# Group norm and key norm of an RWKV-7 layer on one core: head sums as one product with a pair matrix, roots as logarithm and exponential on ScalarE

## The reference

```python
kk = split_heads((k * k_k).astype(f32), N_MAIN_HEADS)
kk = kk * lax.rsqrt(jnp.maximum(jnp.sum(kk * kk, -1, keepdims=True), 1e-24))
...
mean = jnp.mean(y, -1, keepdims=True)
var = jnp.mean(jnp.square(y - mean), -1, keepdims=True)
yn = ((y - mean) * lax.rsqrt(var + GN_EPS)).reshape(bsz, t, D_MAIN)
```

## Time and profile before

| | us |
|---|---|
| median of 3 runs | 3013.67 (3013.06 to 3025.93) |
| the profiled execution | 3011.51 |
| its span in the trace | 3009.5 |
| of this, PE busy | 2826.8 (94%) |
| ACT busy | 1065.8 (35%) |
| DVE busy | 1565.1 (52%) |
| POOL busy | 1209.2 (40%) |

### The profile page before, as it was taken

One profiled execution on the slowest core, in us unless ns is written; L12 is line 12 of the kernel. 1 busy time (PEld: TensorE's weight loads), 2 busy tenths in 40 slices (PEclk: granted clock), 3 DMA queues, 4 the chain that ended last, 5 costly groups with the idle time before them and its releaser, 6 DMA issues. The chain is left out here.

```text
span 3009.5 us, 55580 instructions
## 1 busy us (share of the span) xinstructions
PE 2826.8 (94%) x23253; PEld 2278.6 (76%) x23253; DVE 1565.1 (52%) x2118; ACT 1065.8 (35%) x1870; POOL 1209.2 (40%) x1140
## 2 busy tenths in 40 slices
PE   7999789989879999999999999988889999999998
PEld 6888567777757788888887777756667788888887
DVE  6233456656452754445225778867653745445222
ACT  3111233333232533333103766545543433333000
POOL 6354034444332544444433554432012644444431
PEclk9999789999989999999999999999999999999999
DMA  5332200010032132224423233342122232225321
GB/s 202 108 105 84 98 24 25 24 45 4 3 112 98 57 109 80 80 81 149 140 72 102 57 98 98 114 147 85 64 85 77 63 112 84 85 84 174 106 69 65
DMA packets 265423, 261.21 MB, mean 87 GB/s; under 512 B 9366, under 2 KB 221452, under 8 KB 264024
## 3 DMA queue, kind: packets, MB, share of 16 engines
q1 hardware_dynamic: 258520, 235.50, 24.7%
q10 hardware_dynamic: 6176, 22.13, 2.1%
q0 software_dynamic: 480, 0.03, 0.0%
HBM read 186.80 MB, written 70.83 MB: 86 GB/s over the span
## 5 line engine op out<-in xcount | busy, mean ns | idle before, releaser
L304 POOL TENSOR_TENSOR w_lo_b<-w_raw_b,w_hi_b 128x512 fp32r<-128x512 f32 (+1 forms) x500 | 663.6, 1329 | 520.5 <-ACT w_hi_b L336 506.9
L386 PE MATMUL ps<-b_hi,w_hi_b 128*128 128x512 f32 x1540 | 609.3, 396 | 10.8 <-issue 8.2
L386 PE MATMUL ps<-b_hi,w_lo_b 128*128 128x512 f32 x1540 | 601.5, 391 | 0.0
L386 PE MATMUL ps<-b_lo,w_hi_b 128*128 128x512 f32 x1540 | 601.4, 391 | 0.0
L386 PEld LDWEIGHTS ps<-b_hi,w_hi_b 128*128 128x128 f32 x1540 | 290.7, 189 | 76.9 <-issue 13.7
L386 PEld LDWEIGHTS ps<-b_lo,w_hi_b 128*128 128x128 f32 x1540 | 290.6, 189 | 63.9 <-issue 3.8
L386 PEld LDWEIGHTS ps<-b_hi,w_lo_b 128*128 128x128 f32 x1540 | 290.3, 188 | 60.9
L300 POOL CAST w_hi_b<-w_raw_b 128x384 fp32r<-128x384 f32 (+2 forms) x170 | 99.8, 587 | 492.6 <-PE ps L358 308.4
L336 ACT ACTIVATE w_hi_b<-w_raw_b 128x512 fp32r<-128x512 f32 x330 | 205.9, 627 | 249.4 <-DVE w_raw_b L323 127.4
L358 PE MATMUL ps<-b_hi,w_hi_b 128*128 128x512 f32 x784 | 244.5, 393 | 11.8 <-DVE b_lo L2845 9.0
L358 PE MATMUL ps<-b_lo,w_hi_b 128*128 128x512 f32 x784 | 243.7, 392 | 0.0
(11 more groups left out here) (338 smaller groups left out, 5313.3 us busy)
## 6 DMA issues: line engine op xcount, KB each, us to landing
w_raw_b<-in_w_gate_up SPq DMA_DIRECT2D x88, 512.0 KB, 4.2
act_dram<-x_res SPq DMA_DIRECT2D x44, 512.0 KB, 6.0
stage<-act_dram ACTq DMA_DIRECT2D x32, 512.0 KB, 3.5
w_raw_b<-in_w_down SPq DMA_DIRECT2D x32, 384.0 KB, 3.8
w_raw_a<-in_a_w_in SPq DMA_DIRECT2D x23, 512.0 KB, 4.7
u_dram<-evac_a SPq DMA_DIRECT2D x23, 512.0 KB, 3.0
w_raw_b<-in_w_down SPq DMA_DIRECT2D x32, 320.0 KB, 3.2
w_raw_b<-in_w_out SPq DMA_DIRECT2D x16, 512.0 KB, 5.8
```

The source lines that it names most:

```text
L304: nc.gpsimd.tensor_tensor(self.wlo[:, r, 0:n, :], source, self.whi[:, r, 0:n, :].bitcast(F32), ALU.subtract).then_inc(self.w_lo, 1)
L386: mm = self.nc.tensor.matmul(self.ps[:, bank, :], w[:, r, k, :], h[:, block, k, :], start=(start and k == 0 and a == 0 and h is self.bh), ...
```

## The change

`head_sums` and `spread_half` go. A product with the constant `pairsum` (128x128, one where row and column belong to the same head) gives the sum of squares, already spread over the 64 partitions of its head. The roots become exp(-0.5 ln x) on ACT, over the whole 128x1024 array and not over 16 columns. POOL's power and the two small buffers go.

```diff
@@ PE @@
-                def head_sums(j, to):
-                    for t in range(4 * j, 4 * j + 4):
-                        mm = mmul(to[:, 2 * t:2 * t + 2], sq[:, t * P:(t + 1) * P], self.const("heads"), start=True, stop=True)
-                    return mm
...
+                def kk_product(p, j):
+                    pe.wait_ge(kk_sq, p + 1)
+                    if p and j == 1:
+                        pe.wait_ge(kk_least, 2 * p + 1)
...
+                    side_product(key_sums(p, j), [(self.const("pairsum"), sq[:, at_half(j)])], kk_sum)
...
+                def norm_product(p, j):
...
+                    elif j == 1:
+                        pe.wait_ge(gn_log, 2 * p + 1)
...
+                    side_product(side(j, not last), [(self.const("pairsum"), sq[:, at_half(j)])], gn_sum)
...
                         if now_u:
-                            pe.wait_ge(u_copied, u_count[now_u] - 1)
-                            sums_work(s, l)
                             inverse_u(*now_u)
@@ ACT @@
+                def kk_logs(p, j):
+                    act.wait_ge(kk_least, 2 * p + j + 1)
+                    now = kk[:, p % 2, at_half(j)]
+                    nc.scalar.activation(now, now, ACT.Ln).then_inc(kk_log, 1)
+
+                def kk_roots(p):
+                    act.wait_ge(kk_log, 2 * p + 2)
+                    nc.scalar.activation(kk[:, p % 2, :], kk[:, p % 2, :], ACT.Exp, scale=-0.5).then_inc(kk_root, 1)
+
+                def norm_logs(p, j):
+                    act.wait_ge(gn_sum, 2 * p + j + 1)
+                    nc.scalar.activation(sq[:, at_half(j)], side(j, p < PAIRS - 1), ACT.Ln, scale=1.0 / HD,
+                                         bias=self.const("gn_eps")).then_inc(gn_log, 1)
+
+                def norm_roots(p):
+                    act.wait_ge(gn_log, 2 * p + 2)
+                    nc.scalar.activation(sq[:], sq[:], ACT.Exp, scale=-0.5).then_inc(gn_root, 1)
...
+                    if w < PAIRS:
+                        if r in (8, 9):
+                            kk_logs(w, r - 8)
+                        if r == 9:
+                            kk_roots(w)
...
+                        elif r in (18, 19):
+                            norm_logs(w - 2, r - 18)
+                    if w >= 3:
+                        if r == 0:
+                            norm_roots(w - 3)
+                        elif r == 3:
+                            group_form(w - 3)
@@ DVE side_work @@
                         elif r in (8, 9):
-                            prepare(w, "kk", r - 8)
+                            prepare(w, "kk_least", r - 8)
                         elif r == 10:
+                            prepare(w, "kk")
+                        elif r == 11:
                             prepare(w, "k")
-                        elif r == 11:
-                            prepare(w, "b_decay")
                         elif r == 12:
                             prepare(w, "rk")
                         elif r == 13:
                             prepare(w, "bonus", 0)
-                            prepare(w, "b")
+                            prepare(w, "b_decay")
                         elif r == 14:
                             prepare(w, "bonus", 1)
+                            prepare(w, "b")
...
-                    if 2 <= w <= PAIRS and r == 18:
-                        group_norm(w - 2, "scale", 0)
-                    if w >= 3 and r == 0:
-                        group_norm(w - 3, "scale", 1)
+                    if w >= 3 and r == 2:
+                        group_norm(w - 3, "scale")
```

More of the change, by code:

```diff
@@ L91, in shape_constants @@
     out["ones"] = np.ones((P, 1), np.float32)
+    out["gn_eps"] = np.full((P, 1), GN_EPS, np.float32)
     out["minus_half"] = np.full((P, 16), -0.5, np.float32)
@@ L1361, in phase_rwkv @@
             side = lambda j, alone: ps[:, 7 if alone else 6 + j, :]
-            early_sums = ps[:, 1, 4 * C:4 * C + 16]
-            sums = ps[:, 6, 4 * C:4 * C + 16]
+            rates = lambda p, j: ps[:, 7 if p >= 2 else 6 + j - 2 * p, :]
+            key_sums = lambda p, j: ps[:, 7 if p else j, :]
             window = lambda s: s // STEPS + (2 if s % STEPS == 3 else 1)
@@ L1424, in side_product @@
                     mm.then_inc(semaphore, 1)
-                def head_sums(j, to):
-                    for t in range(4 * j, 4 * j + 4):
-                        mm = mmul(to[:, 2 * t:2 * t + 2], sq[:, t * P:(t + 1) * P], self.const("heads"), start=True, stop=True)
-                    return mm
-                def spread_half(j, bank, roots):
-                    for t in range(4):
-                        for h in range(2):
-                            u = 8 * j + 2 * t + h
-                            mm = mmul(ps[half[h], bank, t * P:(t + 1) * P], roots[:, u:u + 1].broadcast_to([P, HD]), ident, start=True, stop=True)
-                    return mm
                 def decay_product(p, j):
@@ L1704, in _ @@
                 for j in range(2):
-                    norm_sums(PAIRS - 1, j)
-                for j in range(2):
-                    norm_spread(PAIRS - 1, j)
+                    norm_product(PAIRS - 1, j)
             @block.scalar
@@ L1838, in _ @@
                 for j in range(2):
[L1839 removed]
+                    kk_logs(0, j)
+                kk_roots(0)
                 decays(0, 0)
@@ L1847, in _ @@
                 nc.scalar.activation(gate1[:], gate1[:], ACT.Sigmoid).then_inc(gates_ready, 1)
+                for j in range(2):
+                    rate_sigmoid(1, j)
                 tokens(0, 0)
@@ L2089, in _ @@
                 link(nc.vector.memset(chunks(runs[:])[:, :, 0:1], 0.0))
-                prepare(0, "kk_ms")
+                for j in range(2):
+                    prepare(0, "kk_least", j)
                 prepare(0, "scan")
-                for j in range(2):
-                    prepare(0, "kk", j)
+                prepare(0, "kk")
                 for stage in ("k", "rk", "b_decay", "b", "K", "R", "A"):
@@ L2129, in _ @@
                             tail(o, {3: 0, 4: 2, 5: "y"}[l])
-                group_norm(PAIRS - 1, "ms")
-                for j in range(2):
-                    group_norm(PAIRS - 1, "scale", j)
+                group_norm(PAIRS - 1, "scale")
                 group_norm(PAIRS - 1, "bonus")
```

162 lines of the change are left out of this document (46 added, 116 removed).

## The result

The change makes the kernel slower by about half a per cent. Its median is 3031.22 us (8 runs, 3020.68 to 3042.06) beside 3014.74 for the kernel before (8 runs); the ratio is 1.006, with a 95% interval of 1.004 to 1.0079. In a later comparison it was 1.005 (1.0032 to 1.0069). Forecast were 3022.7 us and a loss of 9 us; it lost 16.

A forecast was written before the change was run, and what follows sets the result against it. PE was taken to set the pace (busy 69.25 of 76.00 us per window). Terms -22.7 + 11.2 + 7.7 + 5.75 + 8.5 + 1.5 - 2.9 = +9 on 3011.51, plus 2.2 for the median, gave 3022.7 us; range 2999 to 3040.

The forecast's parts named there:

- Head sums, -22.7: PE loses head sums at r = 5, 6 (10.0 us, windows 2-5) and r = 11, 16 (12.7 us, windows 2-6).
- Key norm, +11.2: r = 8 to 10, windows 2 to 5: ACT's loads and roots delay PE's next piece by 2.8 us each.
- window 1, +7.7: Window 1, from r = 8: key roots behind both decay exponentials delay PE 4.7 us, lower clock adds 3.
- "b" at r = 14, +5.75: DVE's "b" moved from r = 13 delays masks and PE's MV product at r = 15: 1.15 us, windows 1-5.
- Norm product at r = 19, +8.5: PE's second group norm product waits for ACT's load and first logarithm: 1.7 us in windows 2 to 6.
- r = 0 to 3, +1.5: Group norm: existing PE stalls hide ACT's load and exponential; DVE's scaling at r = 2 costs 0.3 us, five times.
- the silent one: r = 0 to 3: PE's existing stalls (1.77 and 3.33 us) were let hide ACT's new work, at no cost.
- Rival 2: r = 9-11, windows 2-5, and r = 19-1: PE stops lower the clock, stalls move; +15 us, 3038; chance 0.21.
- Its sign: Rival 2 would hold if the granted clock falls once a pair.
- End, -2.9: End of the phase, last square to last DVE instruction: 13.6 us before, with POOL's 2.91 us power; 2.9 less.
- Rival 1: r = 8 to 10 and 19: ACT's work hides, only head sums and end count: 2988 us; chance 0.12.
- rival 4: Whole change: removed sums and added waits both fall into idle time, within 3 us of 3014; chance 0.08.

The follow-up runs named there:

- Experiment 6: Changed kernel without the key norm's logarithms and exponential and the group norm's exponential, its logarithm a scaled copy: 3000.95 us, ratio 0.9957 to the kernel before.
- the group norm alone: Kernel before with only the group norm's part of the change, keys as before: 3025.08 us, ratio 1.003.
- the two edits that shorten the idle time: Changed kernel with the second group norm product at r = 0 (3010.51 us), or with the loads of k, v and r spread (3013.91 us).
- first profile: First profiled execution of the changed kernel, nothing altered: 3040.61 us.
- second profile: Second profiled execution of the changed kernel, nothing altered: 3028.74 us.
- key roots spread: Changed kernel with both key logarithms at r = 9, the exponential at r = 10, DVE's key work moved to match: 3024.73 us, ratio 1.0049.
- the loads spread: Changed kernel with the loads of k, v and r issued levels apart, not one right behind the other: 3013.91 us, ratio 1.0007.
- both edits: Changed kernel with the second group norm product at r = 0 and the loads of k, v and r spread: 3004.51 us, ratio 0.9968.

## Why the prediction was right and wrong

The time lay in the range and the direction was right; the 9 us forecast and the 16 measured are made of different parts, though.

- **Head sums, -22.7.** At their places they saved 26.8 (13.8 and 13.0): right, and slightly too small. What the prediction left out is the level behind: 5.6 us at r = 12, 17 and 18 come back, as stops in which PE waits for instructions. Part of them costs nothing in the end, since PE waits less at r = 14.
- **Key norm, +11.2 and window 1, +7.7.** Measured 10.3 and 6.9. The replay of ACT instruction by instruction was within 1 us. In window 1 the clock's part was taken as 3; it is at the lower level for 10.2 us behind the stop of 3.95, 6.8 more than before, so 3.4. Experiment 6 shows that ACT's functions are the cause.
- **"b" at r = 14, +5.75.** Right in sign and too large. The delay shows where it was put: PE waits for DVE's mask behind it for 1.06 us in window 1 and 0.67 in windows 2 to 5, 3.7 in all, and not at all before or in the group norm alone. In windows 2 to 5 it falls behind the copy of r = 15, where the head sums had gone. What made r = 13 to 15 come out at -5.8 was not in the prediction: the wait at r = 14 and the clock behind it, as shown above. The state's chain did not move, for `b_decay`, as long as "b", took its place at r = 13 (DVE, against the earlier trace rows):

```profile
644.98 1.22 DVE L1921 TENSOR_TENSOR a<-a,cum 128x1024 f32<-128x1024 f32 x1
```

- **Norm product at r = 19, +8.5.** Measured 8.7.
- **r = 0 to 3, +1.5.** This is the term that was mis-sized most: 11.9. Its own parts held. ACT's load and exponential cost PE nothing there that experiment 6 can tell (8.3 us with them, 8.8 without, in windows 3 to 6), and the scaling on DVE cost 3.1, inside its bounds. The step that failed is the silent one: that the stalls stay where they are and the clock behind them too. They are PE's wait for instructions; in sum they did not grow (14.6 and 12.9 us), but they stand at other places and in other pieces (in window 3 one of 3.12 us for 1.83 and 1.35), and PE runs at half speed for 20 us more, 10 of the 11.9. Half of that is in window 2, behind a stop of 2.00 us where 1.47 stood. Rival 2 named both halves of this, stalls that move and a clock that falls, with a chance of 0.21; it put 11 of its 15 us at r = 9 to 11, where the clock did not fall, and had it fall behind two stops in one level, which experiment 6 does not bear out. Its sign, the granted clock falling once a pair, was no test: in three of four windows it does so in the kernel before as well, at r = 14. Each of the two edits that shorten the idle time takes the low clock back to about what it was before (10.2 and 13.1 us against 10.2), with the rest of the change in place; why the stalls moved stays open.
- **End, -2.9.** From the end of the last square to the last DVE instruction it was 13.6; now 844.54 to 855.00, 10.5: -3.1.

```profile
844.12 0.42 ACT L1712 ACTIVATE sq_r<-y 128x256 f32<-128x256 f32 x1 [8.32 <-DVE y L2026]
```

```profile
853.78 1.22 DVE L1949 TENSOR_TENSOR x_res<-y,g 128x1024 f32<-128x1024 f32 x1
```

By halves: the keys were forecast at +14.7 and cost 6 to 8, the group norm at -5.6 and cost 9. Two errors of opposite sign, -5.8 for +5.75 at r = 13 to 15 and 11.9 for 1.5 at r = 0 to 4, nearly cancel, so it is partly luck that the total came so close. Rival 1 (ACT's work hides) is out by experiment 6, rival 4 by the table.

Open stays how much of the group norm's loss is the clock. In the profile of the group norm alone the low clock explains 3.4 of the 8.4 us at r = 0 to 4, and DVE's state, later behind the scaling at r = 2, 2.7; for the rest no row was found. Also open is which instructions a fetch must fall on: the changed kernel has 528 products fewer on PE, and a kernel that only adds or removes products was not tried.

## What to carry to other kernels

An idle time of the critical engine that no semaphore explains has to be named before a sum is built on it, for it can move. Put the DMA queues beside it, and if an instruction packet ends just ahead of PE's return and behind a burst of loads, spread the loads; here two waits on SP were worth as much as the whole change cost. Read the granted clock window by window before giving it a cause: half of what was new here lay in a window that the suspected stop does not reach, and only a version without that stop showed that it was not the reason. When a short piece of work is taken out of a long stream of small matrix products, look one level behind for stops of instruction fetch (here 5.6 and 9.1 us for 13 saved), and then at the next wait, which can shrink by the same amount. When two places change at once, as "b" and `b_decay` did, compare with a version in which one of them stayed. And a function with a table load in front, ahead of a copy that PE needs, costs that load on the path even where the engine is idle two thirds of the time.

## What was unexpected of the hardware

- PE's stops for instructions depend on the loads in flight: 3.83 and 1.61 us with 1.5 MB issued at once (two executions), 1.09 with 0.5 MB, at the same product. In 114 of 115 stops of 1 us or more PE goes on 1.19 to 1.60 us after the packet of instructions has ended.
- At one place, the first levels of window 2, stops of 1.75 us (first profile) and 2.00 (second profile, key roots spread) were each followed by 10.2 us at the lower clock, and stops of 1.20 to 1.47 in six other traces by none. Length alone does not settle it: in the group norm alone a stop of 2.85 us in window 4 left the clock at full.
- In the stretch from 410 to 830 us such stops sum up to 21.1 us before, 27.3 and 24.3 in the two profiles of the change, 15.7 with the loads spread and 12.1 with both edits.
- Logarithm and exponential, one behind the other on ACT, each have a load of 1.28 us of their own (L1717 and L1721 above). The Trainium skill ("ScalarE: Activation LUTs", section "Table sets: the hidden batching unit") says that a set with both exists, so that one load would do. This trace does not agree as built: four new loads to a pair stand in it. Two fewer would take 2.6 us a pair off ACT, one of them out of the eight instructions at r = 9.
